# An encoder layer on one core: the sample's first ranking range ends one tile sooner, and the last turn of head outputs stands behind the third ranking round

## The reference, cut to what matters

```
h = rmsnorm(x); u, q, k, v, o, gates = h @ w_in
y = concat(pool_mixer(u), bidirectional_mlstm(q, k, v, o, gates))
x = x + y @ w_out
t = rmsnorm(x)
aff = softmax(t @ w_router)              # rows x 16 experts
gate, idx = top_k(aff.T, cap)            # per expert: 34 rows of the prompt, 130 of the sample
x[idx] += gate * ((silu(t[idx] @ w_gate) * (t[idx] @ w_up)) @ w_down)
y = rmsnorm(x)[16:]
```

## Time and profile before

| | |
|---|---|
| median of 3 runs | 1676.75 us (1674.83 to 1677.18) |
| the profiled execution | 1677.49 us, its span 1675.7 us |
| TensorE busy | 1643.9 us, 98% |
| VectorE, ScalarE, GpSimd busy | 520.0, 397.4, 505.4 us |
| mean granted TensorE clock | 0.996 |

### The profile page before, as it was taken

How to read it: one execution, slowest core, us unless ns; L and a number is a source line. 1 busy time by engine, 2 the same in 40 slices (tenths; PEclk the granted TensorE clock), 3 DMA queues, 4 the chain that set the end, 5 groups by cost and what they waited for, 6 DMA issues and landing times.

```text
span 1675.7 us, 25713 instructions
## 1 busy us (share of the span) xinstructions
PE 1643.9 (98%) x10324; PEld 1413.7 (84%) x10324; DVE 520.0 (31%) x1130; ACT 397.4 (24%) x907; POOL 505.4 (30%) x465
## 2 busy tenths in 40 slices
PE   8999999999999999998999999999999999999996
PEld 5556698876898864455999999999999999999996
DVE  5575344673313661099111110111011110111105
ACT  3335134323222434353011011110111011110115
POOL 0073232632231453342133123322233132322220
PEclk9999999999999999999999999999999999999998
DMA  9311113311111649532688779787788778787794
GB/s 301 95 54 39 38 39 78 97 66 67 39 32 35 199 118 299 149 122 105 236 261 308 245 233 297 247 304 233 239 289 284 268 234 277 247 315 237 233 317 196
DMA packets 199988, 312.98 MB, mean 187 GB/s; under 512 B 23588, under 2 KB 88532, under 8 KB 199664
## 3 DMA queue, kind: packets, MB, share of 16 engines
q1 hardware_dynamic: 182016, 286.45, 49.9%
q0 software_dynamic: 17904, 25.62, 7.6%
HBM read 277.39 MB, written 34.64 MB: 186 GB/s over the span
## 4 chain that ended last, share of the span: by engine, by line
PE 92%; DVE 3%; ACT 2%; issue 1%; POOL 1%; DMA 1%; SPq 0%; DVEq 0%; ACTq 0%; POOLq 0%
PE bank L2558 34%; PE bank L2575 16%; PE bank L2259 9%; PE bank L2286 8%; PE bank L2462 7%; PE bank L2179 3%; PE bank L2215 2%; PE bank L2307 2%; PE bank L2380 2%; PE bank L2361 1%; PE bank L2225 1%; PE bank L2223 1%; PE bank L2595 1%; DVE arena L1941 1%; PE bank L2227 1%
## 5 line engine op out<-in xcount | busy, mean ns | idle before, releaser
L2558 PE MATMUL bank<-arena 128*128 128x164 f32 x4096 | 573.0, 303 | 0.5 <-DVE arena L2050 0.5
L2558 PEld LDWEIGHTS bank<-arena 128*128 128x128 f32 x4096 | 570.8, 190 | 0.7 <-DVE arena L2050 0.7
L2575 PE MATMUL bank<-arena 128*128 128x164 f32 x1920 | 269.6, 303 | 0.0
L2575 PEld LDWEIGHTS bank<-arena 128*128 128x128 f32 x1920 | 268.0, 190 | 0.0
L2060 DVE TENSOR_TENSOR arena<-bank,arena 128x328 f32<-128x328 f32 x64 | 32.0, 500 | 527.5 <-ACT arena L1487 515.3
L1012 POOL DMA_INDIRECT residual<-arena,cur_scatter x90 | 140.8, 1564 | 179.7 <-ACT arena L1498 156.9
L2259 PE MATMUL bank<-arena 128*128 128x400 f32 (+1 forms) x560 | 158.5, 445 | 0.0
L2259 PEld LDWEIGHTS bank<-arena 128*128 128x128 f32 x560 | 106.2, 190 | 51.7
L2462 PE MATMUL bank<-arena 128*128 128x512 f32 x320 | 144.8, 598 | 0.8 <-ACT arena L1347 0.8
L1487 ACT ACTIVATE arena<-bank 128x328 f32<-128x328 f32 x64 | 28.4, 444 | 479.1 <-PE bank L2558 448.4
L2286 PE MATMUL bank<-arena 128*128 128x192 f32 x840 | 137.7, 325 | 0.2 <-ACT arena L1053 0.2
(11 more groups left out here) (280 smaller groups left out, 1586.4 us busy)
## 6 DMA issues: line engine op xcount, KB each, us to landing
arena<-in_w_up SPq DMA_DIRECT2D x32, 2048.0 KB, 14.1
arena<-in_w_down SPq DMA_DIRECT2D x32, 2048.0 KB
arena<-in_w_gate SPq DMA_DIRECT2D x32, 2048.0 KB, 8.0
arena<-in_w_in SPq DMA_DIRECT2D x7, 1536.0 KB, 7.7
arena<-in_x_sample SPq DMA_DIRECT2D x14, 512.0 KB, 6.0
arena<-x_features_first SPq DMA_DIRECT2D x11, 512.0 KB, 7.9
arena<-decay_rows SPq DMA_DIRECT2D x22, 256.0 KB, 4.9
arena<-state_rows SPq DMA_DIRECT2D x44, 128.0 KB, 4.2
```

Of the source, the lines that this page charges most:

```text
L2558: last = pe.matmul(ps[2 * w + fp % 2][:, a * SLOTS:(a + 1) * SLOTS], ring[2 * (fp // 2) + w][:, k, f * P:(f + 1) * P], xeT[:, k, 0:SLOTS], ...
L2575: last = pe.matmul(result_tiles(4 + dp % 2)[:, a, 0:SLOTS], ring[4 + dp // 2][:, k, dt * P:(dt + 1) * P], hidT[:, k, :], start=k == 0, sto ...
```

## The change

`SPLIT` goes from 8 to 7. Everything that is derived from it follows: part 0 of the softmax holds five tiles in place of six, and part 1 four in place of three; `STEP_A` is step 5 in place of 6, for all engines; the ranges are 624 and 416 columns in place of 752 and 288; the affinity groups are 4, 1, 4 and 2 tiles in place of 4, 2, 3 and 2; the prompt's affinities start at column 896 in place of 1024, and the joint rounds pass over 416 columns.

In VectorE's order the last turn moves behind the third round of the first range. All 17 rounds of the first range now stand ahead of the second softmax (before, one of its rounds stood inside it and four behind it), and the scaling of the first range's indices follows them directly. Of the second range, 11 rounds in place of 8 stand ahead of `last_half`, and one in place of four between it and the joint rounds.

```diff
--- before.py
+++ after.py
@@ -58,7 +58,7 @@
 
 ORDER_B = tuple(range(BT, NT)) + tuple(range(BT))
 
-SPLIT = 8
+SPLIT = 7
 STEP_A, STEP_B = SPLIT - BT, NT - BT
 SHORT = ORDER_B.index(NT - 1)
 SOON = (STEP_A, STEP_B)
@@ -2001,23 +2001,20 @@
                     turn_y(j)
                 softmax_first(0, STEP_A - 1)
                 softmax_last(0)
-                turn_y(NT - 1)
                 for g in (0, 1):
                     read_out(dve, ("af", g))
-                rank(0, 0, rounds - 5)
+                rank(0, 0, 3)
+                turn_y(NT - 1)
+                rank(0, 3, rounds)
+                st.do(dve.tensor_scalar(ranked[:, 0, 0:CAP_S], inds[:, 0:CAP_S], float(RANGES[0][0]), None, ALU.add))
                 softmax_first(1, STEP_B - 1)
-                rank(0, rounds - 5, rounds - 4)
                 softmax_last(1)
-                rank(0, rounds - 4, rounds)
                 read_out(dve, ("af", 2))
-                rank(1, 0, JOINT_AT - 4)
+                rank(1, 0, JOINT_AT - 1)
                 last_half()
-                st.do(dve.tensor_scalar(ranked[:, 0, 0:CAP_S], inds[:, 0:CAP_S], float(RANGES[0][0]), None, ALU.add))
-                rank(1, JOINT_AT - 4, JOINT_AT - 2)
+                rank(1, JOINT_AT - 1, JOINT_AT)
                 softmax_first(2, NT - 1)
-                rank(1, JOINT_AT - 2, JOINT_AT - 1)
                 softmax_last(2)
-                rank(1, JOINT_AT - 1, JOINT_AT)
                 read_out(dve, ("af", 3))
                 rank(1, JOINT_AT, rounds, TWO)
```

## The result

The changed kernel took 1680.81 us in the median of 16 runs (1678.50 to 1682.75), the kernel before 1677.08 in 16 runs beside it. The ratio is 1.0023, with a 95% interval of 1.0017 to 1.0030: slower by 3.8 us (the medians differ by 3.7). The profiled execution took 1681.95 us, its span is 1680.1 and its mean granted clock 0.993, for 0.996 before.

The account below looks back on a forecast made before the run. TensorE bounds nearly all, except 751 to 802 us, where the chain runs through VectorE's ranking and joint rounds. Joint rounds starting 0.2 later and taking 1.84 longer give 1676.75 + 2.05 = 1678.8 us; range 1676.2 to 1682.4.

Parts of the forecast that it names:

- The sum: From second softmax through joint rounds: joint rounds start 0.2 us later and take 1.84 us longer, together +2.05 us.
- The moved turn: VectorE's last turn, behind three first-range rounds: its data lands by 712.9 at the worst, so the late turn costs nothing.
- its clockwork from step 7 on is unchanged: TensorE in the projection: the same extra work one step earlier, with the same two short stalls, costed at nothing.
- The term for the clock: TensorE's two longer waits, before last_half's transposes and the index transposes: nothing in the forecast, 0 to 1.7 us each as bounds.
- rival A: Clock falls in one or both longer TensorE waits: 3.75 us slower for one fall, 5.45 for two; chance 0.20.
- The wide range: Whole-kernel time from 1676.2, the runs' lower spread, to 1682.4 us, taking in both falls of the clock.
- the forecast's own range: Whole-kernel time 1677.2 to 1680.3 us, for the spread of runs and 0.5 us of chain errors; forecast chance 0.70.
- the prediction's bound of 0.2%: Whole kernel: 3.4 us, about what a measurement can tell from no change; slower 0.26, same 0.71, faster 0.03.
- Rivals B: Ranking rounds: width costs VectorE next to nothing, a 416-column round takes 1.454 us, total 1674.3 us; chance 0.03.
- C: Late data of the moved turn holds VectorE past the second logits; at 2 us beyond, 1680.8 us; chance 0.04.
- The head start of 7.8 us: First 416-column round starts 7.8 us sooner; three more rounds (5.6) and width (3.2) eat it, so last_half comes 1.0 later.

## Why the prediction was right or wrong

**The sum was right from the second logits on, step by step.** A round took 2.504 us at 624 columns (699.79, then 702.30 and so on) and 1.854 at 416, as interpolated. The moved turn cost nothing, and its data was there. The 416-column rounds started as far ahead of the 288-column ones as said. `last_half` came 1.00 us later by distance (forecast 1.0), the joint rounds without a fall 0.20 later (0.2), the merge 2.06 (2.05). The kernel that has this sum and no fall, with fillers in both waits, measured 1.0014, 2.3 us above before (0.8 to 3.7), beside the 2.05 forecast. From the first expert matmul to the end of the span it is 872.9 to 873.0 us in all thirteen profiles, so the start of the expert layer does reach the end whole.

One small term was put at nothing and was not: "its clockwork from step 7 on is unchanged". The step with the first softmax has five affinity transposes in place of six, and its wait for them is 0.17 in place of 0.25 us; the second logits came 0.2 to 0.3 us sooner. Counted from the projection's first matmul, the trace with both fillers has the merge 1.7 us later than before (182.74 for 181.00), where the forecast has 2.05, and the first expert matmul 1.5 us later. Between merge and first expert matmul lie 9.7 to 10.1 us in the profiles without a fall there; I can't say what makes this difference.

**The term for the clock was mis-sized.** I wrote "I take nothing for it in the sum (the nearest row is the same wait, 1 us shorter)" and gave the falls a chance of 0.20. They are what happens in most executions: of the profiles with a first wait of 3.3 us or more, five in six have a fall behind it, and of those with a second wait of 2.1 us or more, six in seven; 15 of the changed kernel's 28 runs have a mean clock of 0.994 or less. The measured 3.8 us are rival A, which had 0.20 and said 3.75 for one fall and 5.45 for two. That its 3.75 is met so closely is luck: the median is over executions with different numbers of falls, and the single price was off as well. From one stretch of the kernel before I took 1.7 us for a fall. The first one costs 1.0 us on the chain, since only part of the array's work there is on it (3.53 us to the last logits for 2.60); the second costs 1.6 or 2.8 (6.81 and 8.01 for 5.18), as it lies on a filler block which is itself on the chain. The row that misled me was 776 to 780 at 1.00: one execution of one wait. A wait of 2.62 us that goes well once says little about 3.4 us, and the shorter second wait, which I priced but hardly weighed, falls too.

**The wide range held** (1676.2 to 1682.4), since it took in both falls; the forecast's own range (1677.2 to 1680.3) did not, 1680.81 lies 0.5 us above it. By the prediction's bound of 0.2% the measured 0.23% is on the side of slower, which had 0.26, but its interval (0.17 to 0.30%) takes in the bound. Rivals B and C didn't come: the width costs what the slope says, and VectorE still waited 6.81 us ahead of the second softmax; even with the turn ahead of all rounds that softmax was not late.

**What the change could have brought** was hidden by one choice. The head start of 7.8 us was real, and it went into three more rounds ahead of `last_half`. Two of these rounds, put behind it, bring 2.2 us back, and eight more fillers another 2.5 (53.78 to 51.25), which makes it level with the kernel before.

## What to carry to other kernels

Where another engine holds TensorE as long as here (falls came behind single waits of 2.14 us and more), price the wait twice: its own length, and the chance that the clock falls behind it, which here cost about half of the 3.8 us (1.9 between the medians with and without fillers on one chip). A filler count fits the waits of one order of work: 38 left 0.75 us ahead of the index transposes before and 2.22 behind the change. Each reordering has to set it anew. A backlog that is worked off sooner pays only if the operation that others wait for moves ahead with it; count from that operation, not from the engine's total.

## What the runs showed of the hardware that was not expected

Waits of 2.14 us (clock 0.63 and 0.51 behind it), 2.22 (0.54, 0.60) and 2.54 us (0.50 over 796 to 800) were each followed by a fall, and waits of 2.62, 2.26 and 3.42 us in other executions by none. Ahead of the projection two profiles have a fall behind two waits of 1.35 and 0.78 us. Length alone doesn't decide; the same code does both. At the lower level 44 filler matmuls took up to 8.01 us in place of 5.18. The Trainium skill, "TensorE: Matmul & The Clock Gate", section "Why this matters for your kernels", advises to avoid longer idle gaps between matmul bursts; the traces agree that the clock falls behind such gaps, show that it need not (3.42 us without a fall), and show falls behind gaps shorter than the 2.62 us which I had held to be safe. The three passes of a ranking round on 16 partitions follow one line over all four widths seen, 288, 416, 624 and 752 columns: 1.454, 1.854, 2.504 and 2.904 us. On 48 partitions they take 1.46 us at 288 and 1.86 at 416.
